# Two attentions in a hybrid block: score, transpose and P·V work in batches of four units, with four score banks

## The reference, cut to what matters

```python
def dsa_attention(q, k, v, qi, ki, wi):
    ...
        logits = jnp.einsum('bthd,btkd->bhtk', qb, k_g).astype(jnp.float32) * d ** -0.5
        logits = jnp.where(valid[:, None], logits, -1e30)
        p = jax.nn.softmax(logits, axis=-1).astype(v.dtype)
        return jnp.einsum('bhtk,btkd->bthd', p, v_g)
...
def nsa_mixer(h, w_q, q_norm, w_out, shared, cos, sin):
    ...
        s_s = jnp.einsum('bqhgd,bhqkd->bhgqk', qr, ks_g) * scale
        p_s = masked_softmax(s_s, m_s[:, :, None])
        o_s = jnp.einsum('bhgqk,bhqkd->bqhgd', p_s.astype(vs_g.dtype), vs_g)
        ...
        s_w = jnp.einsum('bqhgd,bkhd->bhgqk', qr, kw) * scale
        p_w = masked_softmax(s_w, m_w)
        o_w = jnp.einsum('bhgqk,bkhd->bqhgd', p_w.astype(vw.dtype), vw)
```

## Time and profile before

| | us |
|---|---|
| median of 3 runs | 2139.52 (2138.5 to 2140.99) |
| span of the profiled execution | 2138.8 |
| first attention, `dsa` (from its first scores to the end of P·V) | 205.7 to 255.9 |
| second attention, `nsa` | 1560.5 to 1711.3 |

### The profile page before, as it was taken

How to read it: one execution, slowest core, us unless ns; L and a number is a source line. 1 busy time by engine, 2 the same in 40 slices (tenths; PEclk the granted TensorE clock), 3 DMA queues, 4 the chain that set the end, 5 groups by cost and what they waited for, 6 DMA issues and landing times.

```text
span 2138.8 us, 30783 instructions
## 1 busy us (share of the span) xinstructions
PE 2061.2 (96%) x12072; PEld 1671.2 (78%) x12072; DVE 1257.7 (59%) x2219; ACT 796.7 (37%) x1445; POOL 81.2 (4%) x79
## 2 busy tenths in 40 slices
PE   7999899999999999999999999999889999999998
PEld 6688578888887877787888887889756678888887
DVE  4577757777745449746545446667766856222334
ACT  3323543333424552244222232523456643222222
POOL 1012000000000002000000000001001100000000
PEclk9999899999999999999999999999899999999999
DMA  6321025665432232112656635223200024333221
GB/s 208 98 79 40 14 93 161 199 194 163 163 138 98 80 99 80 63 32 96 205 171 189 203 120 192 94 84 110 89 1 2 2 79 158 99 99 99 99 89 49
DMA packets 146699, 231.49 MB, mean 108 GB/s; under 512 B 7324, under 2 KB 83708, under 8 KB 146556
## 3 DMA queue, kind: packets, MB, share of 16 engines
q1 hardware_dynamic: 144300, 224.05, 32.4%
q0 software_dynamic: 864, 3.15, 0.4%
q10 hardware_dynamic: 1392, 2.33, 0.3%
HBM read 227.41 MB, written 2.10 MB: 107 GB/s over the span
## 4 chain that ended last, share of the span: by engine, by line
PE 84%; DVE 9%; ACT 3%; issue 3%; DMA 1%; POOL 0%; DVEq 0%; SPq 0%; POOLq 0%; ACTq 0%
PE ps L2267 11%; PE ps L2269 11%; PE ps L2268 11%; PE ps L2508 4%; PE ps L2294 4%; PE ps L2296 4%; PE ps L2295 4%; PE ps L2225 4%; PE ps L2227 4%; PE ps L2226 4%; PE ps L2506 3%; PE ps L2580 3%; PE ps L2315 2%; PE ps L2327 2%; PE ps L2340 2%
## 5 line engine op out<-in xcount | busy, mean ns | idle before, releaser
L1564 DVE TENSOR_TENSOR w_lo<-ring,w_hi 128x1024 fp32r<-128x1024 f32 (+4 forms) x362 | 376.8, 1043 | 702.2 <-ACT w_hi L978 700.0
L978 ACT ACTIVATE w_hi<-ring 128x1024 fp32r<-128x1024 f32 (+4 forms) x362 | 329.3, 912 | 970.7 <-PE ps L2269 469.8
L2267 PE MATMUL ps<-x_hi,w_hi 128*128 128x512 f32 x1056 | 416.2, 394 | 0.1
L2269 PE MATMUL ps<-x_hi,w_lo 128*128 128x512 f32 x1056 | 411.2, 389 | 0.0
L2268 PE MATMUL ps<-x_lo,w_hi 128*128 128x512 f32 x1056 | 411.0, 389 | 0.0
L2267 PEld LDWEIGHTS ps<-x_hi,w_hi 128*128 128x128 f32 x1056 | 198.4, 188 | 42.8 <-issue 2.5
L2268 PEld LDWEIGHTS ps<-x_lo,w_hi 128*128 128x128 f32 x1056 | 198.5, 188 | 42.5 <-issue 1.9
L2269 PEld LDWEIGHTS ps<-x_hi,w_lo 128*128 128x128 f32 x1056 | 198.3, 188 | 41.9
L2294 PE MATMUL ps<-w_hi,x_hi 128*128 128x512 f32 x480 | 187.5, 391 | 4.0 <-DVE x_hi L1640 4.0
L2296 PE MATMUL ps<-w_hi,x_hi 128*128 128x512 f32 x480 | 186.8, 389 | 0.0
L2295 PE MATMUL ps<-w_lo,x_hi 128*128 128x512 f32 x480 | 186.8, 389 | 0.0
(11 more groups left out here) (343 smaller groups left out, 3003.8 us busy)
## 6 DMA issues: line engine op xcount, KB each, us to landing
ring<-in_ada_w SPq DMA_DIRECT2D x48, 1024.0 KB, 5.1
ring<-in_ffn_w_in SPq DMA_DIRECT2D x88, 512.0 KB, 4.7
ring<-in_w_up SPq DMA_DIRECT2D x44, 512.0 KB, 4.8
ring<-in_ffn_w_out SPq DMA_DIRECT2D x20, 1024.0 KB, 4.8
ring<-in_hgrn_w_in SPq DMA_DIRECT2D x16, 1024.0 KB, 5.2
ring<-in_w_in SPq DMA_DIRECT2D x12, 1024.0 KB, 5.1
ring<-in_w_down SPq DMA_DIRECT2D x10, 1024.0 KB, 4.9
ring<-in_kv_ada_w SPq DMA_DIRECT2D x8, 1024.0 KB, 5.1
```

Of the source, the lines that this page charges most:

```text
L978: a.activation(to[:, n % depth, 0:src.shape[-1]], src, ACT.Copy).then_inc(s["hi_done"], 1)
L1564: v.tensor_tensor(to[:, n % depth, 0:width], src, hi[:, n % depth, 0:width].bitcast(F32), ALU.subtract).then_inc(s["lo_done"], 1)
L2267: mm(bs[j], wh[:, k, c], x_hi[:, 2 * q + k], start=first, stop=False)
L2269: ins = mm(bs[j], wl[:, k, c], x_hi[:, 2 * q + k], start=False, stop=last)
```

## The change

`plan_attention` gives scores four banks (0 to 3, by `i % 4`), transposes and returns together a ring of three banks (4, 5, 6, in the order of their use), and outputs one (7). The last return of an attention gets a bank that suits the stage after it.

PE goes in steps of four units: four scores of batch j, four transposes of batch j − 1, the return B of a finished group in each odd step from the third on, and the four P·V of batch j − 1. DVE does three logits of batch j, then its copies of batch j − 1, then the fourth logits, and in odd steps `finish`. ACT does its copy of the first unit of batch j − 1, an exponential of batch j, its copy of the third unit, the other three exponentials, and in even steps the copy of an output bank.

Who copies is set by the new `by_act`: above 256 keys ACT has the even units, as before; at 256 keys ACT has the first pair of a batch and DVE the second (before, DVE had both); at 128 keys DVE has both, as before.

```diff
@@ -364,22 +364,34 @@
             return n <= 2 * P
+        def by_act(i, n):
+            return i % 2 == 0 and (n > 2 * P or n == 2 * P and i % 4 == 0)
         def t_key(name, i, n):
             return (name, "T", i - i % 2 if copied_together(n) else i)
         def plan_attention(name, n_units, width):
-            for i in range(n_units):
-                plan_bank((name, "S", i), i % 2)
-                if copied_together(width(i)):
-                    if i % 2 == 0:
-                        plan_bank((name, "T", i), 2 + i // 2 % 2)
-                else:
-                    plan_bank((name, "T", i), 2 + i % 2)
-            for g in range(n_units // 8):
-                plan_bank((name, "O", g), 4 + g % 2, counted=False)
-                plan_bank((name, "B", g), 6 + g % 2)
+            at = [0]
+            def in_turn(key):
+                plan_bank(key, 4 + at[0] % 3)
+                at[0] += 1
+            for j in range(n_units // 4 + 2):
+                for i in range(4 * j, min(4 * j + 4, n_units)):
+                    plan_bank((name, "S", i), i % 4)
+                for i in range(4 * j - 4, min(4 * j, n_units)):
+                    if i >= 0 and (i % 2 == 0 or not copied_together(width(i))):
+                        in_turn((name, "T", i))
+                if j == n_units // 4 + 1:
+                    plan_bank((name, "B", (j - 3) // 2), (turn[0] + 4) % 8)
+                elif j >= 3 and j % 2:
+                    in_turn((name, "B", (j - 3) // 2))
+                if j % 2 and j < n_units // 4:
+                    plan_bank((name, "O", j // 2), 7, counted=False)
@@ -1062,37 +1074,49 @@
             def attention(name, between):
                 unit_of, n_units, (L, PB, PT, OT), base = ATT[name]
-                for i in range(n_units + 8):
-                    if i < n_units:
...
+                def exponent(i):
+                    if i >= n_units:
+                        return
+                    if between:
+                        between(i)
...
+                for j in range(n_units // 4 + 1):
+                    pt_out(name, 4 * j - 4, n_units)
+                    exponent(4 * j)
+                    pt_out(name, 4 * j - 2, n_units)
+                    for i in range(4 * j + 1, 4 * j + 4):
+                        exponent(i)
+                    if j and j % 2 == 0:
+                        g = j // 2 - 1
                         act.wait_ge(s["pv_done"], base + 8 * (g + 1))
                         if g >= 2:
                             filled(act, (name, "B", g - 2))
                         p = ps[:, bank_use[name, "O", g][0]]
                         a.activation(OT[:, g % 2], p, ACT.Copy).then_inc(free((name, "O", g)), 1)
-            def pt_out(name, i):
+            def pt_out(name, i, n_units):
                 unit_of, _, (_, _, PT, _), base = ATT[name]
+                if i < 0 or not (by_act(i, unit_of(i)["n"])):
+                    return
                 n = unit_of(i)["n"]
                 if i >= 4:
-                    act.wait_ge(s["pv_done"], base + i - 3)
+                    act.wait_ge(s["pv_done"], base + i - (2 if copied_together(n) else 3))
                 p = filled(act, (name, "T", i))
-                a.activation(PT[:, i % 4, 0:n], p[:, 0:n], ACT.Copy).then_inc(free((name, "T", i)), 1)
+                if copied_together(n):
+                    a.activation(PT[:, i % 4:i % 4 + 2, 0:n], p[:, 0:2 * n].rearrange("p (q n) -> p q n", q=2), ACT.Copy)\
+                        .then_inc(free((name, "T", i)), 1)
+                else:
+                    a.activation(PT[:, i % 4, 0:n], p[:, 0:n], ACT.Copy).then_inc(free((name, "T", i)), 1)
@@ -1674,29 +1698,42 @@
             def attention(name, bias_ready, finish):
                 unit_of, n_units, (L, PB, PT, _), base = ATT[name]
-                for i in range(n_units + 8):
-                    if i < n_units:
...
+                def logits(i):
+                    if i >= n_units:
+                        return
...
+                def turned(i):
+                    n = unit_of(i)["n"]
+                    if by_act(i - 1 if copied_together(n) else i, n):
+                        return
+                    if i >= 4:
+                        dve.wait_ge(s["pv_done"], base + i - 3)
+                    key = t_key(name, i, n)
+                    pt = filled(dve, key)
+                    if copied_together(n):
+                        v.tensor_copy(PT[:, (i - 1) % 4:i % 4 + 1, 0:n], pt[:, 0:2 * n].rearrange("p (q n) -> p q n", q=2))\
+                            .then_inc(free(key), 1)
+                    else:
+                        v.tensor_copy(PT[:, i % 4, 0:n], pt[:, 0:n]).then_inc(free(key), 1)
+                for j in range(n_units // 4 + 2):
+                    for i in range(4 * j, 4 * j + 3):
+                        logits(i)
+                    if 1 <= j <= n_units // 4:
+                        turned(4 * j - 3)
+                        turned(4 * j - 1)
+                    logits(4 * j + 3)
+                    if j >= 3 and j % 2:
+                        finish((j - 3) // 2, base)
@@ -2307,14 +2344,14 @@
             def attention(name, turn_half):
                 unit_of, n_units, (L, PB, PT, OT), base = ATT[name]
-                for j in range(n_units // 2 + 4):
-                    if 2 * j < n_units:
-                        pair = [unit_of(2 * j + q) for q in range(2)]
-                        banks = [open_bank((name, "S", 2 * j + q)) for q in range(2)]
+                for j in range(n_units // 4 + 2):
+                    for i in range(4 * j, min(4 * j + 4, n_units), 2):
+                        pair = [unit_of(i + q) for q in range(2)]
+                        banks = [open_bank((name, "S", i + q)) for q in range(2)]
                         for q in range(2):
                             mm(banks[q][:, 0:pair[q]["n"]], pair[q]["q"], pair[q]["k"], start=True, stop=True)\
-                                .then_inc(full((name, "S", 2 * j + q)), 1)
-                    for i in (2 * j - 4, 2 * j - 3):
+                                .then_inc(full((name, "S", i + q)), 1)
+                    for i in range(4 * j - 4, 4 * j):
                         if 0 <= i < n_units:
                             u = unit_of(i)
                             pe.wait_ge(s["p_ready"], base + i + 1)
@@ -2327,8 +2364,18 @@
                                 ins = tr(b[:, at + c:at + c + P], PB[:, i % 4, c:c + P], ident)
                             if second or not copied_together(n):
                                 ins.then_inc(full(key), 1)
-                    i = 2 * j - 6
-                    if 0 <= i < n_units:
+                    if j >= 3 and j % 2:
+                        g = (j - 3) // 2
+                        if g == n_units // 8 - 1:
+                            turn_half()
+                        b = open_bank((name, "B", g))
+                        evacuated(pe, (name, "O", g))
+                        for c in range(4):
+                            ins = tr(b[:, c * P:(c + 1) * P], OT[:, g % 2, c * P:(c + 1) * P], ident)
+                        ins.then_inc(full((name, "B", g)), 1)
+                    for i in (4 * j - 4, 4 * j - 2):
+                        if not 0 <= i < n_units:
+                            continue
                         pair = [unit_of(i + q) for q in range(2)]
                         b = open_bank((name, "O", i // 8)) if i % 8 == 0 else ps[:, bank_use[name, "O", i // 8][0]]
                         for q in range(2):
@@ -2341,15 +2388,6 @@
                                          start=(c == 0), stop=(c == nb - 1))
                                 if c == nb - 1:
                                     ins.then_inc(s["pv_done"], 1)
-                    if j >= 7 and j % 4 == 3:
-                        g = (j - 7) // 4
-                        if g == n_units // 8 - 1:
-                            turn_half()
-                        b = open_bank((name, "B", g))
-                        evacuated(pe, (name, "O", g))
-                        for c in range(4):
-                            ins = tr(b[:, c * P:(c + 1) * P], OT[:, g % 2, c * P:(c + 1) * P], ident)
-                        ins.then_inc(full((name, "B", g)), 1)
```

53 lines of the change are left out of this document (16 added, 37 removed).

## The result

The changed kernel takes 2125.97 us (median of 4 runs, 2125.37 to 2126.86) against 2139.01 us before (4 runs, 2137.31 to 2140.99): a ratio of 0.994, 95% interval 0.9928 to 0.9953. Measured a second time, beside other kernels, it took 2127.01 against 2140.2, ratio 0.9941 (0.9929 to 0.9953). 13 us are gone, 0.6% of the whole.

What follows compares the result with a forecast made beforehand. PE, busy 96% of 2138.8 us, was taken as the bound, except DVE early in the first attention. Gains of 8.0 + 3.1 + 3.0 = 14.1 us took the median 2139.5 to 2125.4, stated as 2126, range 2120 to 2131.

Steps and rivals of the forecast that it cites:

- Fewer phases: PE, both attentions: three phase entries per four units, not six, save at most 1.17 us a group, 18.7 in the second.
- Hand-over: Second attention: P·V waits for copies out of PSUM, leaving gains of 0.74, 0.59, 0.67 and 0 a group, 8.0 us.
- Where it waits: PE idle before P·V, after ACT's or DVE's copy: about 0.4 us per step at 256 and 128 keys, 0.1 to 0.2 above.
- Fill and drain: Second attention: four score banks bring the first P·V after 7.0 us, not 10.4, gaining 3.1; the end unchanged, 0.
- First attention: About 1.5 us less up to 239.7, then 0.7 from merged steps and 0.8 from a shorter tail: together 3 us.
- The copies' split: At 256 keys half of the 512-column copies go from DVE to ACT, costing nothing beside the stall.
- The profiled span: Whole profiled execution: 14.1 us off 2138.8, which gives 2124.7 us.
- The first: Rival, every width: the hand-over takes all back, leaving the fill and half the first attention's gain; 2135 us, chance 0.13.
- The second: Rival, all widths: no hand-over counts and the ceiling is met; 2115 us, chance 0.12.
- The third: Rival, first attention: 3 us slower, as DVE waits once a batch for copy, P·V and scores; 2131 us, chance 0.13.
- fourth: Rival, first attention: PE's half clock lasts to its end, 19 us lost, 14 gained; 2145 us, chance 0.05.
- The fifth: Rival, PE: banks or merged phases don't do what they say, fill and phase rows stay; 2139.5 us, chance 0.05.

Runs made afterwards that it cites:

- score_banks: The kernel before, its order kept, with four score banks in place of two and returns sharing the outputs' two banks: 2135.56 us, ratio 0.9975.
- act_last: Changed kernel with one ring of seven banks; at 384 and 512 keys ACT copies second and fourth units, ahead of its exponentials: 2118.58 us, ratio 0.9891 to before.
- scores_split: Changed kernel with the second score pair between transposes and products at 128 and 256 keys, in steps without returns: 2121.11 us, ratio 0.9904 to before.

## Why the prediction was right

It said 2126 us, and 2125.97 was measured. The mechanism held, but that the two agree to 0.03 us is luck: the working gave 2125.4, an allowance of 0.6 for a cost that turned out to be nothing was added, and several terms were off by 0.3 to 2 us and cancelled. By its own steps:

- **Fewer phases, ceiling 1.17 a group.** Right. Four scores take 1.92 us, with no second entry, so the part that I had left open as 0.06 or 0.21 a step is nothing. That the entries are the price is shown from both sides: with the banks alone (score_banks) the groups stay at 13.01 and 10.49 us; with the phases merged and the waits taken away (act_last) they are 11.90 and 9.41, 1.11 and 1.08 less.
- **Hand-over.** The sum of 8.0 us is right, its parts are not, which is luck. The groups gained 0.65, 0.45, 0.44 and 0.47 us from 512 to 128 keys, where 0.74, 0.59, 0.67 and 0 stood: four times each is 8.05. At 256 keys and up the waits were underestimated by 0.1 to 0.2. At 128 keys the term that failed is "DVE starts its next step late": the logits after a finish start 0.71 us after their scores (1683.72 to 1684.43), only 0.2 later than in the step without one (0.52), and the step after the returns takes 2.67 us, not 3.0. The two errors cancelled; the size of each width was right only to 0.2 us, at 128 keys to 0.5.
- **Where it waits.** Named rightly (ACT's copy at 256, DVE's at 128 keys, the ring above), but at 512 keys I put 0.19 us on a step without B, and the trace has about 0.15 in the transposes and 0.14 in P·V. One late bank is paid for twice. With one ring the second payment goes, and the second attention is 4.1 us shorter, 0.6 of it in the fill. ACT's margin held: its copy of the third unit ends at 1593.91, and the P·V pair that needs it starts at 1594.43.
- **Fill and drain.** First P·V after 7.0 us, as forecast (7.03). Of the second attention's 10.7 us, 2.6 is left beside the 8.05 for the fill and the ends, where I had 3.1. The drain, put at 0, costs 0.65 (3.35 us for 2.70).
- **First attention.** 3.0 forecast, 2.6 measured, inside the bounds. Cut at the second return, the front part gives 1.3 us (1.5 forecast) and the end 1.4 (0.7 and 0.8 forecast), so both halves of the working hold. How much of the front part is the clock is open: PE's mean grant in the stretch from 205 to 256 us was 0.83 before and 0.87 after.
- **The copies' split.** Costed at nothing beside the stall, which holds. That it also gains was not in the sum: without it the groups at 256 keys take 7.70 and not 7.38 us, 1.3 us in all.
- **The profiled span.** 2124.7 forecast, 2123.5 found, with 13.3 us from the attentions and 2.0 from between them. The clock ahead of the second attention was granted differently in every profile (0.78 before, 0.85 and 0.81 in the changed kernel's two), so I don't count these 2 us as the change's. Without them the span would be 2125.5, 0.8 us above the forecast.

None of the rivals is what the change did. The first (the hand-over takes all back) is out, since every width gained; it comes true with two transpose banks, where the group at 512 keys takes 13.39 us. The second (no wait counts) is out, since 12.36 us isn't 11.84; act_last comes near to it at 512 and 384 keys. The third and fourth are out, since the first attention is shorter and the clock is 0.98 from 223.6 and 1.00 from 239.7. The fifth is out by the phase rows and the fill.

## What to carry to other kernels

When phases of different tile shapes alternate on PE, read the price of entering a phase from two widths of the same loop, and the ceiling follows. Then write down, for each wait that the merging adds, when it is released: by the place of the releasing instruction in its engine's queue, and not only by its duration. Here a bank that came free late was paid for again where its contents were used. Give the phases one common ring in the order in which they are filled before tuning who does the copies, because the same exchange of copies gained 0.8 us with the ring and lost 4.2 without it. And before a change of a few us is believed, look at the lengths of the stages in the trace: the median of scores_split fell by 7 us more than its attentions became shorter.

## What the runs showed of the hardware

- PE enters a phase of four score tiles at the price of one entry: 1.92 us, against 2 × 1.06 for two phases of two.
- Entering a phase of another tile shape costs 0.15 to 0.21 us here, worked out from phases of 128 and 512 keys, and merging phases took a group of eight units from 13.01 to 11.90 us when the waits were gone too.
- A PE phase with a wait of 0.15 us inside doesn't look idle in the profile. Its busy time reads 2.12 instead of 1.97 us, and only the distance of the starts and the weight loads show the wait.
- TensorE's granted clock differs between two executions of the same kernel: over 1515 to 1560 us it was 0.85 and 0.81 in the changed kernel's two profiles, and the second attention began at 1555.74 and 1556.77. Between variants it was 0.83 to 0.93 over 205 to 256 us, with first attentions of 49.9 and 46.9 us.
